# Second attention of a two-block kernel: two heads and one branch in a step, values kept stationary

## The chip, the cores and the metric

The kernel runs on one NeuronCore of a Trainium2 chip. The metric is the device time of one execution in microseconds (us). Four compute engines and a DMA system work side by side and meet only at semaphores: TensorE (PE, matrix products and transposes into the PSUM banks), VectorE (DVE), ScalarE (ACT) and GpSimd (POOL); SyncE (SP) issues the weight transfers. Each engine runs its own instructions strictly in the order in which they are written.

## The reference, cut to what matters

A first block (gated scan, attention, 16-expert layer) feeds a second block, and only the attention of the second block is touched. It works on 512 tokens with 8 query heads in 2 groups, 64 wide. Each head has three branches over the same queries: `cmp` over 31 compressed keys, `slc` over selected blocks (with 8 blocks and a top of 16, all causal keys), and `win` over a window of 512 (again all causal keys here). Scores get a distance penalty with one slope for each head, then a masked softmax, and each branch is weighted by a gate:

```python
s = jnp.einsum('bgrqd,bgqmd->bgrqm', qb, kg).astype(f32)
p_slc = masked_softmax(s - slopes * dist, dist >= 0)
o_slc = jnp.einsum('bgrqm,bgqmd->bgrqd', p_slc.astype(vg.dtype), vg)
...
o = gb[..., 0:1] * o_cmp + gb[..., 1:2] * o_slc + gb[..., 2:3] * o_win
...
mixed = jnp.concatenate([rms_norm_2(attn_out, g_out[l, :ATTN_WIDTH]),
                         rms_norm_2(conv_out, g_out[l, ATTN_WIDTH:])], axis=-1)
x = x + mixed @ w_o[l]
```

## The kernel before, in words

Everything is written by hand for each engine: `pe`, `act`, `dve`, `pool`, `sync` hold one nested function for each stage, and the stages follow one another as `second` (projections and the gated convolution), `select` (the second attention) and `ffn` (output projection `wo2`, then the feed-forward layer).

`second` computes 12 column tiles of the convolution (keys `("conv", c)`), each 24 matmuls on TensorE (L565), each with its weights split into two parts by ACT (`copy_hi`, L946) and DVE (`sub_lo`, L1415). Between them, `after` on DVE applies the norms: of the keys at tiles 0 and 1, of the queries at tiles 8 and 9.

`select` first transposes queries and keys, compresses the keys (`blkT`, L755 to L786), and then runs 32 steps, one for each block `i` of 128 queries (from the last, which sees 512 keys, to the first, which sees 128) and each head `h`. `select_order` sets for all engines where the pieces of a step stand: scores of step n, transposes of step n - 2, values of step n - 3, and at certain steps the compressed branch, the norm of the convolution (`mix_conv`) and the turning of a finished block (`turn_out`). One step is:

- PE: two matmuls (one for each branch v) of `q2T` against `kz2`, in which the other group's half is zeros (L772).
- DVE: adds slope times distance for each branch (L1954) and takes the negative row maximum (L1958).
- ACT: two exponentials with row sums (L1302).
- PE: 2(i + 1) transposes of the weights (L342); ACT copies them out (L1343).
- PE: 2(i + 1) matmuls with the transposed weights stationary and 128 value columns moving (L346).
- DVE: reciprocal of the sum times the gate (L2033, L2035) and two accumulations into `o2` (L2044).

After the eighth head of a block DVE norms the block (L2051 to L2059, with a square root on ACT), PE transposes it and DVE writes it to `mixT`, the input of `wo2`. `ffn` starts only when all three engines have ended `select`. In the text, "block" means such a block of 128 queries, called by its i.

The PSUM has 8 banks; `Banks(lo, hi)` hands them out in turn, and a taker waits for the reader of the former content.

Of the kernel before, what the change touches and what calls it, by code (L numbers as in the profile page):

```python
# [17 lines left out]
EPS = 1e-6  # L18
# [58 lines left out]
class Ring:  # L77


    def __init__(self, tensor, sems, units):  # L80
# [4 lines left out]
        for name, _, k, n in units:  # L85
            slots = [(at + s) % NS for s in range(1 if k * n <= 2048 and k <= 4 else 2)]
            at += len(slots)
            count[slots[0]] += 16
# [17 lines left out]
def cols(w, a, n):  # L106
    return w[:, a:a + n].rearrange("(k p) n -> p k n", p=128), w.shape[0] // 128, n


def weight_units(d):  # L110
# [15 lines left out]
    for p in range(8):  # L126
        for name in ("gate", "up", "down"):
            for kq in range(4):
                for e2 in range(2):
                    w = d["w_exp_" + name][2 * p + e2].rearrange("(p k) n -> p k n", k=8)  # L130
                    u.append(((name, p, kq, e2), w[:, 2 * kq:2 * kq + 2, :], 2, 1024))
# [4 lines left out]
    u += [(("wo2", s), *cols(d["w_o_2"], 512 * s, 512)) for s in range(2)]  # L136
# [12 lines left out]
def program(nc, d, out):  # L149
# [81 lines left out]
    kz2 = Area(nc, HT, DYN).take("kz2", [128, 2, 2, 512])  # L231
    m10 = Area(nc, DYN + 5216, END)
    q2T, hdn = m10.take("q2T", [128, 4, 512]), m10.take("hdn", [128, 2, 256])
    hdk, kcm = m10.take("hdk", [128, 256]), m10.take("kcm", [32, 2, 128])
    kcz, tA2 = m10.take("kcz", [128, 2, 32]), m10.take("tA2", [128, 128])
    p2, st2 = m10.take("p2", [128, 4, 2, 512]), m10.take("st2", [128, 6, 3, 2])
    cst, on = m10.take("cst", [128, 3, 8]), m10.take("on", [128, 1])
    blkT = Area(nc, m10.at, END).take("blkT", [128, 16, 2, 2, 32])
    p2T, cp = m10.take("p2T", [128, 2, 2, 512]), m10.take("cp", [128, 8, 32])
    cpT, o2 = m10.take("cpT", [32, 8, 128]), m10.take("o2", [128, 2, 512])  # L240
    o2n = m10.take("o2n", [128, 512])
# [77 lines left out]
    sec_chunks += col_chunks(("conv",), lambda u: ("conv", u), 12, 4)  # L319
    ffn_chunks = col_chunks(("wo2",), lambda u: ("wo2", u), 8, 4)  # L320
# [17 lines left out]
    def pe(T):  # L338
# [27 lines left out]
        def setup():  # L366
            b = every.take(T, "cols", dve_in["colB"])
            T.wait_ge(s_ident, 16)
            T.wait_ge(s_rows, 16 * 14)
# [187 lines left out]
        def chunk_tile(pool, key, wR, chunks, n, x, nk, freed, ready=None):  # L557
# [3 lines left out]
            for k in range(nk):  # L561
                if ready:
                    T.wait_ge(*ready(k))
                for j, (s, t) in enumerate(TERMS):
                    mm = T.matmul(b, o[s][:, k, :], x[:, t, k, :], start=(k + j == 0), stop=(k == nk - 1 and j == 2))  # L565
# [7 lines left out]
        def mix():  # L573
# [10 lines left out]
            for n, (key, *_) in enumerate(mix_chunks):  # L584
                if key[0] == "gate":
# [5 lines left out]
                    chunk_tile(pool, key, wR1, mix_chunks, n, hR1, 8, dve_mix["silu", h],  # L591
                               (lambda k: dve_mix["hR", k]) if h == 0 else None)
                elif key[0] == "mg":
                    chunk_tile(pool, key, wR1, mix_chunks, n, hR1, 8, act_mix["mg", key[1], key[2]])
                elif key[0] == "wb":
# [3 lines left out]
                    chunk_tile(pool, key, wR1, mix_chunks, n, aR, 4, dve_mix["wb", br, t])  # L599
# [3 lines left out]
                else:  # L603
# [4 lines left out]
                    chunk_tile(pool, key, wR1, mix_chunks, n, hR1, 8, dve_mix["y", t])  # L608
# [95 lines left out]
        def second():  # L704
            pool = Banks(0, 8)
            for n, (key, *_) in enumerate(sec_chunks):
                if key[0] == "raw":
                    v = key[1]
                    chunk_tile(pool, key, wR2, sec_chunks, n, hR2, 8, dve_sec["raw", v],
# [7 lines left out]
                elif key[0] == "conv":  # L717
                    chunk_tile(pool, key, wR2, sec_chunks, n, hR2, 8, dve_sec["conv", key[1]])
# [17 lines left out]
        def select():  # L736
            pool = Banks(0, 8)
            T.wait_ge(*dve_sec["qn", 1])
            for i in range(4):
                b = pool.take(T, ("q2T", i), act_sel["q2T", i])  # L740
# [3 lines left out]
            for v, src in enumerate((ksw, kww)):  # L744
                b = pool.take(T, ("k2T", v), act_sel["k2T", v])
                for i in range(4):
                    mm = turn(b[:, 128 * i:128 * i + 128], src[:, i, 0:128])
                mm.then_inc(pe_sel.sem, pe_sel.up(("k2T", v)))
            T.wait_ge(*dve_sel["blk"])
            b = pool.take(T, "hdk", act_sel["hdk"])  # L750
# [9 lines left out]
            b = pool.take(T, "hdn", act_sel["hdn"])  # L760
            T.wait_ge(*act_sel["hdk"])
            for hh in range(2):
                mm = turn(b[:, 128 * hh:128 * hh + 128], hdk[:, 128 * hh:128 * hh + 128])
# [1517 lines left out]
```

## Time and profile before

| | us |
|---|---|
| median of 3 runs | 2099.91 (2099.75 to 2102.64) |
| the profiled execution | 2094.38 |
| its span, first to last instruction | 2093.1 |
| the stretch 1481.58 to 1677.15: `select` and the first tile of `wo2` | 195.57 |
| TensorE busy over the span | 1808.2 (86%) |
| DVE / ACT busy over the span | 866.0 (41%) / 547.3 (26%) |

The profile is of one execution; its instructions carry the line of the program that wrote them. TensorE's busy time counts an instruction from its start to its modelled end, so neighbours overlap. The granted clock is 1.00 at 2.4 GHz and 0.50 at 1.2 GHz.

### The profile page before, as it was taken

The numbers are of one execution on the slowest core, as the hardware profiler recorded it, in microseconds if no ns is written. First come the engines' busy times: TensorE is split into PE (matmuls) and PEld (weight loads), VectorE is DVE, ScalarE is ACT, GpSimd is POOL, SyncE is SP. The second block draws the span as 40 slices with busy tenths as digits, with TensorE's granted clock in tenths as the row PEclk, the third lists the DMA queues.
The fourth block names the chain that finished last, engine by engine and source line by source line (L and its number), as shares of the span: only waits on it lengthen the run. The fifth ranks groups of instructions, "written<-read, shape, count | busy, mean of one in ns | idle before, by whom it ended". The sixth has DMA issues, their size and how long they took to land.

```text
span 2093.1 us, 21196 instructions
## 1 busy us (share of the span) xinstructions
PE 1808.2 (86%) x8537; PEld 1227.8 (59%) x8537; DVE 866.0 (41%) x1365; ACT 547.3 (26%) x908; POOL 126.8 (6%) x120
## 2 busy tenths in 40 slices
PE   4999889897899893888888888899788699999998
PEld 2657475766677771333232333488467678888876
DVE  4066372437733426011110111527567744444443
ACT  2134333334522313000000000232345533222221
POOL 0002120203000001000000000000000001000010
PEclk9999999998999996999999999999889899999999
DMA  9131202112104221999999999442300022232211
GB/s 348 55 109 41 82 20 101 41 72 90 41 1 167 104 98 52 384 421 421 421 422 422 421 420 420 150 156 85 121 1 1 1 81 81 82 120 81 81 41 41
DMA packets 92360, 329.44 MB, mean 157 GB/s; under 512 B 7348, under 2 KB 22632, under 8 KB 67688
## 3 DMA queue, kind: packets, MB, share of 16 engines
q1 hardware_dynamic: 84384, 312.59, 38.1%
q10 hardware_dynamic: 5928, 8.16, 1.2%
q0 software_dynamic: 1952, 7.34, 0.9%
q8 instruction: 69, 1.13, 0.2%
q14 instruction: 27, 0.22, 0.0%
HBM read 322.82 MB, written 4.19 MB: 156 GB/s over the span
## 4 chain that ended last, share of the span: by engine, by line
PE 66%; DMA 14%; DVE 12%; ACT 4%; issue 3%; ACTq 1%; POOL 1%; SPq 1%; DVEq 0%; POOLq 0%
PE PS L565 20%; PE PS L346 13%; PE PS L663 8%; PE PS L884 8%; DMA ring<-in_w_exp_down_dram 6%; DMA ring<-in_w_exp_gate_dram 5%; PE PS L342 3%; PE PS L534 3%; PE PS L674 2%; PE PS L729 2%; DVE wR L1415 1%; PE PS L772 1%; PE PS L426 1%; DMA ring<-in_w_mod_dram 1%; DVE mrow L1426 1%
## 5 line engine op out<-in xcount | busy, mean ns | idle before, releaser
L565 PE MATMUL PS<-hR,wR 128*128 128x512 f32 x1200 | 301.0, 410 | 30.9 <-DVE wR L1415 17.1
L565 PEld LDWEIGHTS PS<-hR,wR 128*128 128x128 f32 x1200 | 233.8, 197 | 95.6 <-issue 34.5
L663 PE MATMUL PS<-ring,xeT 128*64 128x512 f32 x1024 | 230.3, 600 | 40.3 <-DMA ring<-in_w_exp_gate_dram 38.0
L1415 DVE TENSOR_TENSOR wR<-ring,wR 128x1024 fp32r<-128x1024 f32 (+2 forms) x142 | 161.1, 1135 | 250.8 <-ACT wR L946 250.6
L946 ACT CAST wR<-ring 128x1024 fp32r<-128x1024 f32 (+2 forms) x142 | 138.3, 975 | 217.0 <-PE PS L884 126.5
L663 PEld LDWEIGHTS PS<-ring,xeT 128*64 128x64 f32 x1024 | 76.8, 138 | 192.5 <-issue 186.1
L884 PE MATMUL PS<-wR,hR 128*128 128x512 f32 x768 | 176.2, 390 | 8.9 <-DVE tmp L2097 6.9
L565 PE MATMUL PS<-xR,wR 128*128 128x512 f32 x768 | 175.3, 389 | 0.0
L884 PEld LDWEIGHTS PS<-wR,hR 128*128 128x128 f32 x768 | 143.6, 188 | 41.5 <-DVE tmp L2097 9.6
L565 PEld LDWEIGHTS PS<-xR,wR 128*128 128x128 f32 x768 | 144.1, 188 | 29.9
L663 PE MATMUL PS<-ring,hidT 128*64 128x512 f32 x512 | 115.2, 596 | 25.9 <-DMA ring<-in_w_exp_down_dram 20.0
L346 PE MATMUL PS<-hT,ring 128*128 128x512 f32 (+1 forms) x320 | 111.8, 508 | 4.2 <-ACT KK L1046 4.2
L663 PEld LDWEIGHTS PS<-ring,hidT 128*64 128x64 f32 x512 | 38.0, 137 | 97.9 <-issue 90.2
L346 PE MATMUL PS<-ring,hT 128*128 128x256 f32 (+1 forms) x352 | 90.5, 418 | 1.0 <-DVE hT L1475 1.0
L346 PEld LDWEIGHTS PS<-hT,ring 128*128 128x128 f32 x320 | 60.3, 190 | 53.0 <-issue 46.3
L346 PEld LDWEIGHTS PS<-ring,hT 128*128 128x128 f32 x352 | 66.6, 190 | 23.8 <-issue 15.3
L1207 ACT ACTIVATE hid<-PS 128x1024 f32<-128x1024 f32 x8 | 8.2, 1024 | 275.5 <-PE PS L663 275.5
L1832 DVE TENSOR_TENSOR hid<-hid,PS 128x1024 f32<-128x1024 f32 x8 | 9.8, 1221 | 159.5 <-ACT hid L1207 159.5
L1844 DVE TENSOR_SCALAR ye<-PS,giT 128x512 f32<-128x512 f32 x16 | 11.3, 746 | 151.4 <-PE PS L663 151.4
L2190 POOL TENSOR_TENSOR tmp<-tmp 128x512 f32<-128x512 f32 x32 | 33.3, 1042 | 524.0 <-DVE tmp L2097 524.0
L1562 DVE TENSOR_REDUCE st<-PS 128x1 f32<-128x768 f32 x32 | 30.6, 955 | 81.4 <-PE PS L427 81.4
L534 PE MATMUL PS<-Y 128*128 128x128 f32 x448 | 57.9, 285 | 6.9 <-DVE Y L1662 6.8
(381 smaller groups left out, 2316.9 us busy)
## 6 DMA issues: line engine op xcount, KB each, us to landing
ring<-in_w_exp_gate_dram SPq DMA_DIRECT2D x64, 1024.0 KB, 13.9
ring<-in_w_exp_up_dram SPq DMA_DIRECT2D x64, 1024.0 KB, 13.7
ring<-in_w_exp_down_dram SPq DMA_DIRECT2D x64, 1024.0 KB, 11.9
ring<-in_w_mod_dram SPq DMA_DIRECT2D x12, 2048.0 KB, 8.6
ring<-in_w_in_dram SPq DMA_DIRECT2D x11, 2048.0 KB, 9.3
ring<-in_w_up_dram SPq DMA_DIRECT2D x8, 2048.0 KB, 8.3
ring<-in_w_down_dram SPq DMA_DIRECT2D x8, 2048.0 KB, 7.8
ring<-in_w_in_dram SPq DMA_DIRECT2D x9, 1024.0 KB, 5.5
```

The costliest lines, as they stand in the source:

```text
L342: return T.transpose(dst, src, ident[0:k, 0:k])
L346: mm = T.matmul(dst, l, r, start=(i == 0), stop=(i == len(pairs) - 1))
L534: mm = T.matmul(b[:, 128 * x:128 * x + 128], yy, yy, start=True, stop=True)
L565: mm = T.matmul(b, o[s][:, k, :], x[:, t, k, :], start=(k + j == 0), stop=(k == nk - 1 and j == 2))
L663: mm = T.matmul(b[es, ns], stat[:, 2 * kq + k, es], W.view(units[e2])[:, k, ns], start=(kq + k == 0), stop=(kq == 3 and k == 1))
L674: T.matmul(b, ye[:, p % 2, 128 * k:128 * k + 128], PT[:, p % 2, :], start=True, stop=True) \
L729: mm = T.matmul(bs[i][:, 0:cs.stop - cs.start], hR2[:, s, kk + k, 128 * i:128 * i + 128], o[t][:, k, :], start=(kk + k + j == 0), stop=(kk ...
L884: mm = T.matmul(down[m], uR[:, r % 2, s, k, 128 * i:128 * i + 128], o[t][:, 0, 512 * q:512 * q + 512], start=(k + j == 0), stop=(k == 3 an ...
L946: A.copy(parts(wR, chunks, n)[0], W.view(unit)[:, ks, cs]).then_inc(act_hi.sem, act_hi.up(key))
L1415: V.tensor_tensor(lo, W.view(unit)[:, ks, cs], hi.bitcast(F32), ALU.subtract) \
L1562: V.tensor_reduce(st[:, n % 4, 0:1], bank(("s", n))[:, 0:768], AX, ALU.max, negate=True) \
L2190: G.tensor_tensor(tmp[:, j, :], tmp[:, j, :], tmp[:, j, :], ALU.mult) \
```

## The change

The 32 steps of `select` are made of other pieces. A step m is now a block i, a pair of heads (j of group 0 and j of group 1) and one branch v:

- PE: two matmuls with 64 contraction rows each, one for each group, on the two halves of the partitions (`kT2` without zeros), and two matmuls that add slope times distance (`slopes`, `distR`, single-pass type F32R) into the same banks. A step takes two of four banks (`four`), so two steps are in flight, and a bank pair is free when ACT has taken the exponentials.
- DVE: the maximum straight from PSUM, then, a step later, `scale`: the weights are multiplied by gate over sum before they are transposed.
- PE: the transposes as before; ACT copies them out, DVE every second one of branch 1 (half of that branch's).
- PE, once for each block: `values2`, 4(i + 1) matmuls with 64 value columns stationary and 512 columns (four heads of 128 queries) moving, plus two of the compressed branch, all summed in one bank.
- The norm over a finished block is a sum of squares on PE (`square2`); its reciprocal root is multiplied in by POOL at the end, after the last block.

`mix_conv` moves ahead of the compression; the compressed branch is asked for at other steps; the norm of the queries goes from tiles 8 and 9 to 2 and 3; `g_out` is loaded by two transfers and `wo2` by three for each unit (another order of rows); `wo2` takes the convolution's tiles first, and its first weights are split within `select`.

```diff
 def select():  # pe
...
+            def scores(m):
+                i, j, v = sel_steps[m]
                 nk = 128 * (i + 1)
+                b = four.take(T, ("s2", m), act_sel["e", m], 2)
+                for g in range(2):
+                    gs = slice(64 * g, 64 * g + 64)
+                    T.matmul(b[:, 512 * g:512 * g + nk], q2T[gs, j, 128 * i:128 * i + 128], kT2[gs, v, 0:nk],
+                             start=True, stop=False)
+                for g in range(2):
+                    mm = T.matmul(b[:, 512 * g:512 * g + nk], slopes[:, 4 * g + j, :], distR[:, 512 - nk:512],
+                                  start=False, stop=True)
+                mm.then_inc(pe_sel.sem, pe_sel.up(("s", m)))
...
+            def values2(m):
+                i = sel_steps[m][0]
+                b = pool.take(T, ("o2", i), dve_sel["mx", i])
                 T.wait_ge(*dve_sel["cpT", i])
...
                     for c in range(i + 1):
+                        for g in range(2):
+                            mm = T.matmul(b[64 * g:64 * g + 64, :], vt[:, c, 128 + 64 * g:192 + 64 * g],
+                                          pT2[v][:, c, g].rearrange("p j q -> p (j q)"), start=False,
+                                          stop=(v == 1 and c == i))
+                mm.then_inc(pe_sel.sem, pe_sel.up(("o", i)))
...
+    def select_order(scores, compress1, compress2, compress3, compressed1, compressed2, turn2, values2, square2):
+
+        for m in range(36):
+            if m < 32:
+                scores(m)
+            if m < 3:
+                (compress1, compress2, compress3)[m]()
+            if m >= 3 and (m - 3) % 8 == 7:
+                values2(m - 3)
+            if 2 <= m < 34:
+                turn2(m - 2)
+            if m < 32 and m % 8 == (3 if m < 8 else 1):
+                compressed1(sel_steps[m][0])
+            if m < 32 and m % 8 == (6 if m < 8 else 5):
+                compressed2(sel_steps[m][0])
+            if m >= 4 and (m - 4) % 8 == 7:
+                square2(sel_steps[m - 4][0])
...
-                    if c in (8, 9):
-                        if c == 8:
+                    if c in (2, 3):
+                        if c == 2:
                             V.wait_ge(*act_sec["q", 3])
...
+            def scores(m):
+                nk = 128 * (sel_steps[m][0] + 1)
+                V.wait_ge(*pe_sel["s", m])
+                V.tensor_reduce(st2[:, m % 4, 0, :], bank(("s2", m)).rearrange("p (g x) -> p g x", g=2)[:, :, 0:nk], AX,
+                                ALU.max, negate=True).then_inc(s.sem, s.up(("max", m)))
+                if m:
+                    scale(m - 1)
+
+            def scale(m):
...
+                for g in range(2):
+                    p = p2[m % 4][:, g, 0:nk]
+                    V.tensor_scalar(p, p, r[:, g:g + 1], None, ALU.mult).then_inc(s.sem, s.up())
+                s.also(("sc", m))
...
+            def values2(m):
...
+                V.wait_ge(*act_sel["sqa", i])
+                V.tensor_tensor(mixT[:, 0:4, 128 * i:128 * i + 128],
...
+    sel_steps = [(i, j, v) for i in range(3, -1, -1) for j in range(4) for v in range(2)]
```

On TensorE, in the middle of `select`, before the change, block i = 3 (`p` weights, `p2T` their transposes, `ksw` and `kww` the two branches' values):

```order
L772 MATMUL PS<-kz_143,q2T 128x512 x2
L342 MATMUL PS<-ident,p_150 128x128 x8
L346 MATMUL PS<-ksw,p2T 128x128 x4
L346 MATMUL PS<-kww,p2T 128x128 x4
L772 MATMUL PS<-kz_143,q2T 128x512 x2
L342 MATMUL PS<-ident,p_150 128x128 x8
```

The same engine after the change, where block 3 ends and block 2 has begun (`q_135` and `p2b` are the weights' buffers, `pT_148` and `pT_149` their transposes by branch):

```order
L825 MATMUL PS<-kcT,q2T 128x32 x8
L790 MATMUL PS<-kT_143,q2T 128x384 x2
L793 MATMUL PS<-distR,slopes 128x384 x2
L851 MATMUL PS<-cpT,kcm 64x512 x2
L859 MATMUL PS<-pT_148,ksw 64x512 x8
L859 MATMUL PS<-pT_149,kww 64x512 x8
L356 MATMUL PS<-ident,q_135 128x128 x6
L790 MATMUL PS<-kT_143,q2T 128x384 x2
L793 MATMUL PS<-distR,slopes 128x384 x2
L356 MATMUL PS<-ident,q_135 128x128 x6
L868 MATMUL PS<-sq,ones 128x128 x4
```

The values have gone out of the steps into one run of 18 matmuls, which stands between the scores of two steps of the next block.

On DVE, before, the end of a block (block 3's norm stands between two steps of block 2):

```order
L2044 SCALAR_TENSOR_TENSOR o_158<-PS,st_151,o_158 128x64 x2
L2051 TENSOR_TENSOR o2n<-o_158 128x512
L2053 TENSOR_REDUCE on<-o2n 128x1
L2055 TENSOR_SCALAR on<-on 128x1
L2057 RECIPROCAL on<-on 128x1
L2059 TENSOR_SCALAR o2n<-o_158,on 128x512
L1954 SCALAR_TENSOR_TENSOR p_150<-dist,PS 128x384 x2
L1958 TENSOR_REDUCE st_151<-p_150 128x2
```

On DVE after, the same place:

```order
L1978 TENSOR_REDUCE st_153<-PS 128x2
L1988 RECIPROCAL st_153<-st_153 128x2
L1990 TENSOR_TENSOR st_153<-st_153,gat 128x2
L1995 TENSOR_SCALAR q_135<-q_135,st_153 128x384 x2
L2074 TENSOR_TENSOR mixT<-PS,colA 128x4x128
L1978 TENSOR_REDUCE st_153<-PS 128x2
L1988 RECIPROCAL st_153<-st_153 128x2
L1990 TENSOR_TENSOR st_153<-st_153,gat 128x2
L1995 TENSOR_SCALAR p2b<-p2b,st_153 128x384 x2
L2064 COPY pT_149<-PS 128x3x128
L2081 TENSOR_SCALAR rinv<-PS 128x128
```

The five instructions of the norm are gone; the block's `mixT` product (L2074) stands ahead of the next step's maximum.

## Rows read from the trace of the kernel before

**Rows 1.** Busy time in the stretch: us, PE, PEld, DVE, ACT, POOL, PEclk, DMA, GB/s.

```profile
1481.58:1677.15 195.57, 152.90 (x924) 121.79 (x923) 128.43 (x324) 95.36 (x248) 0.15 (x1) 0.87 0.07 25
```

**Rows 2.** Chain that ended last, block 3: start us, us, what.

```profile
1532.33 1.72 PE PS L772 x4
1534.05 0.87 PE PS L342 x8
1534.92 1.79 PE PS L346 x16
```

**Rows 3.** A low and a high stretch; TensorE's longest wait (us, times, longest).

```profile
1508.00:1512.00 4.00, 2.52 (x12) 2.52 (x13) 0.00 (x0) 1.41 (x6) 0.00 (x0) 0.50 0.25 92
...
1588.00:1636.00 48.00, 43.22 (x317) 37.98 (x315) 38.56 (x109) 27.06 (x85) 0.00 (x0) 1.00 0.00 1
...
PE PS L342 <- DVE o2n L2059: 11.6, 4, 3.9
```

**Rows 4.** Timeline of TensorE in the experts: start us, us, line, operation, tiles.

```profile
999.45 2.74 PE L663 MATMUL PS<-ring,hidT 128*64 128x512 f32 x12
1003.29 1.08 PE L663 MATMUL PS<-ring,hidT 128*64 128x512 f32 x4 [1.10 <-DMA ring<-in_w_exp_down_dram]
```

**Rows 5.** Timeline of TensorE where a 31-row product meets a full-size one.

```profile
1576.27 1.99 PE L823 MATMUL PS<-kcm,cpT 31*128 31x64 f32 x16
...
1578.20 0.87 PE L342 MATMUL PS<-ident,p 128*128 128x128 f32 x6
```

**Rows 6.** Groups of 1480 to 1670: shapes xcount, busy us, mean ns, idle before.

```profile
L1302 ACT ACTIVATE p<-p,st 128x512 f32<-128x512 f32 x16 | 11.4, 714 | 25.2 <-DVE st L1958 25.2
...
L1958 DVE TENSOR_REDUCE st<-p 128x2 f32<-128x1024 f32 x8 | 9.8, 1220 | 0.3
...
L2033 DVE RECIPROCAL st<-st 128x2 f32<-128x2 f32 x32 | 4.9, 154 | 0.0
...
L1958 DVE TENSOR_REDUCE st<-p 128x2 f32<-128x256 f32 x8 | 3.4, 420 | 0.3
...
L2059 DVE TENSOR_SCALAR o2n<-o,on 128x512 f32<-128x512 f32 x4 | 1.9, 486 | 0.1
...
L1978 DVE TENSOR_SCALAR rinv<-PS 128x512 f32<-128x512 f32 x1 | 0.7, 692 | 7.6 <-PE PS L796 7.6
```

**Rows 7.** The same view for the first attention, whose operands lie in PSUM.

```profile
L1017 ACT ACTIVATE pb<-PS,st 128x768 f32<-128x768 f32 x32 | 28.9, 902 | 79.0 <-DVE st L1562 79.0
...
L1562 DVE TENSOR_REDUCE st<-PS 128x1 f32<-128x768 f32 x32 | 30.6, 955 | 81.4 <-PE PS L427 81.4
```

**Rows 8.** Chain through the compressed branch of block 3, first and last pieces.

```profile
1513.21 0.43 DVE cp L1998
...
1516.56 0.43 DVE cp L2018
...
1519.44 1.13 DVE cpT L2024
```

**Rows 9.** Chain: the compression, and the convolution's sum of squares.

```profile
1487.63 8.84 PE PS L755 x64
...
1547.00 5.30 PE PS L796 x8
```

**Rows 10.** Timeline from the end of `select` into `wo2`.

```profile
1666.90 1.04 ACT L946 CAST wR<-ring 128x1024 fp32r<-128x1024 f32 x1 [2.39 <-DVE mixT L1989]
...
1668.08 1.23 DVE L1415 TENSOR_TENSOR wR<-ring,wR 128x1024 fp32r<-128x1024 f32 x1 [1.34 <-ACT wR L946]
...
1670.05 12.51 PE L565 MATMUL PS<-hR,wR 128*128 128x512 f32 x48 [4.04 <-DVE hR L2073]
```

**Rows 11.** Timeline of TensorE in convolution tiles 10 and 11.

```profile
1467.49 7.33 PE L565 MATMUL PS<-hR,wR 128*128 128x512 f32 x24 [2.28 <-DVE wR L1415]
...
1475.81 5.73 PE L565 MATMUL PS<-hR,wR 128*128 128x512 f32 x24 [1.00 <-DVE wR L1415]
```

**Rows 12.** Chain at the start: issues of the small loads on ACT's queue.

```profile
5.89 0.34 ACTq L956
```

More of the change, by code:

```diff
@@ L560, in chunk_tile @@
             o = parts(wR, chunks, n)
-            for k in range(nk):
+            for k in ks:
                 if ready:
@@ L748, in select @@
                 mm.then_inc(pe_sel.sem, pe_sel.up(("k2T", v)))
+            b = early.take(T, "vc2", dve_sel["vc2"])
+            for k in range(4):
+                T.wait_ge(*act_sel["vc2", k])
+                T.matmul(b, ones, sq[:, k % 2, :], start=(k == 0), stop=(k == 3)) \
+                    .then_inc(pe_sel.sem, pe_sel.up(("vc2", k)))
             T.wait_ge(*dve_sel["blk"])
-            b = pool.take(T, "hdk", act_sel["hdk"])
+            b = early.take(T, "hdk", act_sel["hdk"])
             for v in range(2):
@@ L848, in ffn, with square2 @@
+            def square2(i):
+                b = pool.take(T, ("tot2", i), dve_sel["tot", i])
+                T.wait_ge(*act_sel["sqa", i])
+                for j in range(4):
+                    mm = T.matmul(b[:, 0:128], ones, sq[:, i % 2, 128 * j:128 * j + 128], start=(j == 0), stop=(j == 3))
+                mm.then_inc(pe_sel.sem, pe_sel.up(("tot", i)))
+            select_order(scores, compress1, compress2, compress3, compressed1, compressed2, turn2, values2, square2)
         def ffn():
@@ L1350, in select, with turn2 @@
-            select_order(scores, compress2, compress3, mix_conv, lambda i: None, compressed, turn2, values2)
+            def turn2(m):
+                i, j, v = sel_steps[m]
+                if i < 3 and j + v == 0:
+                    A.wait_ge(*pe_sel["o", i + 1])
+                for g in range(2 - v):
+                    A.wait_ge(*pe_sel["pT", m, g])
+                    A.copy(pT2[v][:, 0:i + 1, g, j, :],
+                           bank(("pT2", m, g))[:, 0:128 * i + 128].rearrange("p (c q) -> p c q", q=128)) \
+                        .then_inc(s.sem, s.up(("pT", m, g)))
@@ L2061, in select, with turn2 @@
-            select_order(scores, compress2, compress3, mix_conv, turn_out, compressed, lambda n: None, values2)
+            def turn2(m):
+                i, j, v = sel_steps[m]
+                if m == 30:
+                    scale(31)
+                if v:
+                    if i < 3 and j == 0:
+                        V.wait_ge(*pe_sel["o", i + 1])
+                    V.wait_ge(*pe_sel["pT", m, 1])
+                    V.tensor_copy(pT2[1][:, 0:i + 1, 1, j, :],
+                                  bank(("pT2", m, 1))[:, 0:128 * i + 128].rearrange("p (c q) -> p c q", q=128)) \
+                        .then_inc(s.sem, s.up(("pT", m, 1)))
@@ L2181, in pool @@
             gather(p)
-        G.wait_ge(*dve_sec["qn", 0])
-        G.memset(kz2, 0.0).then_inc(pool_sec.sem, pool_sec.up("kz2"))
         for g in (pe_mm[("conv", 11), 0], act_sec.end, dve_sec.end):
             G.wait_ge(*g)
-        G.memset(kcz, 0.0).then_inc(pool_sec.sem, pool_sec.up("kcz"))
+        for h in range(8):
+            G.tensor_scalar(slopes[:, h, :], ident, float(np.float32(2.0 ** -(h + 1))), None, ALU.mult) \
+                .then_inc(pool_sec.sem, pool_sec.up())
+        pool_sec.also("slopes")
+        G.wait_ge(*dve_sel["n2"])
+        for j in range(4):
+            G.tensor_tensor(mixT[:, j, :], mixT[:, j, :], rinv, ALU.mult).then_inc(pool_ffn.sem, pool_ffn.up(("n2", j)))
         for r in range(8):
```

411 lines of the change are left out of this document (175 added, 236 removed).

## The prediction

> **What bounds the kernel now.** I read the granted clocks first (one core), then the chain of work that ended last, then the timeline from the last convolution tile to the first tile of the output projection, because only that stretch is rewritten: 1481.58 to 1677.15, 195.6 us [rows 1]. In it TensorE is busy 152.9 us, DVE 128.4, ACT 95.4, and the mean granted clock is 0.87 [rows 1]. With two levels, 0.50 and 1.00, that is 26% of the stretch, some 51 us, at 1.2 GHz. In block 3 (512 keys) the chain stays on TensorE: 1.72 us of scores, 0.87 of transposes, 1.79 of values, 4.38 us a step [rows 2]. What breaks this are waits of TensorE at the ends of the blocks: 11.6 us in four waits for the normed block, up to 3.9 us long [rows 3]. After such waits the clock is low: 1508 to 1512, behind a wait for the compressed keys, ran at 0.50 [rows 3]. So the stretch is bound by TensorE's work in its first half, by chains through DVE at the block ends, and by the low clock behind them.
>
> **The change, TensorE's work.** The price of two half-size matmuls comes from the experts, where two 64-column products also share the array: 12 instructions in 2.74 us, and four alone, the first after a wait, in 1.08 [rows 4]. A float32 matmul is two instructions, so one of 512 columns costs 0.457 us in such a run, where a full-size one takes 1.72 / 2 = 0.86 [rows 2]. No row shows two products on the two halves of the *rows*; they could overlap likewise (0.91 us a pair) or not at all (1.72). I take 0.91, as the column pairs are the nearest row. The distance products are single-pass: 24 in 5.73 us at the full clock [rows 11], 0.24 each, 0.48 a step; new work. Transposes stay at 0.87. A step of block 3 then asks 0.91 + 0.48 + 0.87 = 2.26 us of TensorE in place of 4.38. The values come as one run for each block of 4(i + 1) + 2 matmuls: 18, 14, 10, 6 times 0.457 = 8.2, 6.4, 4.6, 2.7 us.
>
> **DVE becomes the bound of a step.** The two slope additions and two accumulations go; a maximum over 1024 numbers costs 1.22 us from SBUF [rows 6], and PSUM as source is no dearer (768 numbers 0.955 us [rows 7], against 0.95 between the two sizes of L1958). Then a reciprocal 0.154, a product of the same size, two multiplications of 512 columns at 0.486, and half a copy of 512 columns out of PSUM, for which I take the 0.69 of L1978 [rows 6]: 1.22 + 0.31 + 0.97 + 0.35, and five gaps of 0.04, 3.04 us. ACT needs 2 x 0.71 and one and a half copies, at 0.69 like DVE's, 2.46 [rows 6], and exponentials from PSUM are no dearer (768 columns 0.90 [rows 7]). The loop through two score buffers (scores 1.39, maximum 1.22, exponentials 1.42, some 4.2 us for two steps) is shorter than two DVE steps. So a step is 3.04 us, and for 384, 256 and 128 keys, with the multiplications taken linearly between 0.15 and 0.486 and the maximum between 1.22 and 0.42, it is 2.54, 2.05, 1.53. Eight of each: **73.3 us**.
>
> **What stands between the steps.** The compressed branch is three plus six small DVE instructions, 1513.21 to 1516.99 with 0.45 on ACT [rows 8], so 3.3 on DVE; then DVE waits in its order for eight transposes of TensorE (0.9) and copies 1.2 [rows 8]: 5.5 a block, **22**. The score maxima queued behind wait all that time, and TensorE for some 4.3 us of it. The values: DVE has one maximum and one `scale` left when the run begins (2.4, 2.1, 1.6 us), then waits for the run, ACT's square and its own `mixT` product, since the next maximum is queued behind: 5.8 + 4.3 + 3.0 of wait and 1.0 each for product and mean, **16**. The head: the squares' matmuls move ahead of the compression (four of 0.86 through two buffers behind ACT's copies, to about 1490.5, where the compression started at 1487.63 before); 64 compression instructions need 6.9 us at the full clock (8.84 with its low start [rows 9]); scores 1.4. **16.5** from 1481.58 to the first maximum. In return the 5.30 us run with its 4.2 us wait at 1547 [rows 9] is gone. The compressed keys' chain still delays steps 1 and 2: **4**. The tail: last transposes and copies 2.2, values 2.7, square 0.6, weight split 1.04 and 1.23 [rows 10], a quarter of a reciprocal 0.9, a difference 0.6, 24 matmuls 5.5: **14.7**. POOL's four products of 1.04 us each stand behind the convolution's tiles, which `wo2` now takes first; without that cover they would cost 4 us. Sum at the full clock: 73.3 + 22 + 16 + 16.5 + 4 + 14.7 = **147 us**.
>
> **The low clock.** TensorE keeps one wait of about 4.3 us in each block (the compressed branch), one in the head, one in the tail, and has less work between. I take as much time at 1.2 GHz as now, 50 us. There a step of block 3 takes 4.5 in place of 3.04, of block 2 3.4 in place of 2.54, of block 1 2.3 in place of 2.05, of block 0 no more; runs of values, head and tail double. About a third of 50 us is lost: **17**. The stretch becomes 164 us, a gain of 31.6. The bounds are 0 us (full clock) and 72 (all low: 20 for the steps, 22 for the values, 30 for the rest).
>
> **The edits outside.** The query norms leave DVE at convolution tiles 8 and 9, where TensorE waits 2.28 and 1.00 us and one tile runs 7.33 in place of 5.5 [rows 11], 5.1 us in all. At tiles 2 and 3 each adds 5.9 us to 1.9 of DVE work where a tile lasts 5.5; the slack there is some 2 us, so tile 5 waits about 2.7, perhaps with a low clock behind. Between 0 and 2.4 gained; I take **1**. The extra transfer of `g_out` costs one issue of 0.34 us [rows 12], and the first weight transfer waits for the last of these loads: **0.35 lost**. The additional `wo2` transfers are issued 150 us ahead of their use and cost nothing; were they late they would cost an issue of 0.4 us each, four times.
>
> The sum: 31.6 + 1 - 0.35 = 32 us. Against the profiled execution (2094.4, of which the span is 2093.1) that gives 2062; that execution ran 5.5 below the median, so against the median of 2099.9 it is **2068**.
>
> **A rule against it.** In front of and behind a product of 31 rows nothing shows: 16 instructions start 1.93 us ahead of the next full-size one [rows 5], 0.12 each, as among themselves. The Trainium skill, "TensorEngine Tiling (Array Packing)", Key Properties, says that changing the tiling mode drains the TensorE; the new step changes it twice. By the rows the sum stays at 2068; by the rule it would be the drain rival below.
>
> **The rivals.**
> - *Drain at each change of tile size.* Speaks for it: 64 changes and more, where before only the compressed branch had any. Against: [rows 5]. If a change costs the 0.15 us by which an instruction's 0.27 exceeds its 0.12 pitch, up to 10 us come on TensorE; DVE's slack hides most, 2 to 9 are left: 2070 to 2077, **2074**. 8%.
> - *The clock hardly falls.* Steps keep TensorE at work three quarters of the time, and from 1588 to 1636, TensorE being busy 43 of 48 us, the clock stayed at 1.00 [rows 3]. 147 us: **2051**. 12%.
> - *The halves don't overlap.* A step of block 3 needs 3.07 us of TensorE, equal to DVE's, some 5 us over all; 48 matmuls of values cost 0.86, 19 us more. 171 and 14 for the clock: **2089**. Against it: the experts [rows 4]. 9%.
> - *Slower: the clock stays at 1.2 GHz.* Waits in every step keep TensorE from its full clock. The stretch is 147 + 72 = 219 us: **2123**. It decides from two thirds of the stretch at 0.50 (147 + 72 x 0.67 = 195.6); before it was a quarter. Against: the value runs of up to 8 us, in which nothing waits. 5%.
>
> **How the numbers follow.** The forecast itself, with its own 2058 to 2079 (10 to 27 us lost to the clock), has 66%. The range reaches from the full clock, with some of DVE's multiplications cheaper than taken, 2048, to just past the rival without overlap, 2090. About 0.2% (4 us) is what a measurement here can tell from no change; only a mixture of lost overlap and low clock lands there, 2%; slower 5%; faster 93%.
>
> **What would show it.** Right: a step of block 3 about 3.0 us from maximum to maximum with DVE busy throughout; value runs of 8.2 us; the first `wo2` tile ending 164 us after the convolution; mean clock about 0.85 there; waits of DVE for `sqa` near 5.8 us. Wrong: pairs of 64-row products at 1.7 us; maxima from PSUM above 1.3; a mean clock below 0.7; a wait for POOL's `slopes` or `n2`.

## The result and the profile after

The changed kernel takes 2069.07 us (median of four, 2061.46 to 2070.81) against 2101.27 before: 0.9848 of the time, 95% interval 0.9829 to 0.9867. 2068 was predicted. Run once more beside the last experiments it took 2072.03 (2069.30 to 2075.02) against 2096.34 for the kernel before, 0.9883 [0.9862, 0.9904]: 24 us less there, where the first comparison has 32. The executions lie apart with the clock: 2061.5 came with a mean granted clock of 0.958, 2075.0 with 0.950. One execution each of two kernels below was in a slower state and is in no median or bracket: 3686.5 us (fillers in the blocks alone) and 2211.0 (values split). The profiled execution is the one of 2061.46 us, span 2060.1.

The rewritten stretch, from the last convolution tile to the first addition behind the first `wo2` tile, in the view of rows 1 (length, busy PE, PEld, DVE, ACT, POOL, clock, DMA, GB/s), first in this profile, then in the later one:

```profile
1480.41:1643.96 163.55, 135.08 (x716) 75.39 (x714) 110.36 (x261) 78.57 (x221) 11.85 (x12) 0.84 0.08 29
```

```profile
1483.26:1652.36 169.10, 142.19 (x716) 78.51 (x714) 110.44 (x262) 78.80 (x221) 11.83 (x12) 0.80 0.08 28
```

195.6 us at 0.87 [rows 1] have become 163.6 at 0.84. TensorE lost 18 us of work there, DVE 18. On TensorE the saving lies in the values: their matmuls (L346 and L823 before, L851 and L859 after) fell from 60.4 us of busy time to 25.8, while scores with the distance rose from 44.6 (L772) to 50.1 (L790 and L793). An undisturbed step of block 3 on DVE, timeline of the profile after (start, us, engine, line, operation, tiles):

```profile
1521.14 1.22 DVE L1978 TENSOR_REDUCE st<-PS 128x2 f32<-128x1024 f32 x1
1522.28 0.15 DVE L1988 RECIPROCAL st<-st 128x2 f32<-128x2 f32 x1
...
1522.66 0.88 DVE L1995 TENSOR_SCALAR q<-q,st 128x512 f32<-128x512 f32 x2
1523.46 0.68 DVE L2064 COPY pT<-PS 128x512 f32<-128x512 f32 x1
1524.14 1.23 DVE L1978 TENSOR_REDUCE st<-PS 128x2 f32<-128x1024 f32 x1
```

The maximum from PSUM costs 1.22, as from SBUF [rows 6]. But each instruction begins before the listed end of the one ahead: 1.14 behind the maximum's start, 0.80 behind that of two multiplications. Steps alternate between 2.32 us and, with a copy, 3.00: 2.66 on average. TensorE, same stretch and view:

```profile
1516.34 1.11 PE L790 MATMUL PS<-kT,q2T 64*128 64x512 f32 x4
1517.38 0.74 PE L793 MATMUL PS<-distR,slopes 128*128 128x512 f32 x2
1517.99 1.06 PE L356 MATMUL PS<-ident,p2b 128*128 128x128 f32 x8
1518.98 1.13 PE L790 MATMUL PS<-kT,q2T 64*128 64x512 f32 x4
```

From start to start: 1.04 for the pair of scores, 0.61 for the distance, 0.99 for the transposes, 2.64 together. So the halves do share the array (1.04, not 1.72), and TensorE needs as much as DVE. TensorE at the compressed branch and in the value run of block 3 (at the end of a row, how long it stood and for whom):

```profile
1528.58 1.87 PE L356 MATMUL PS<-ident,cp 128*32 128x128 f32 x8 [3.60 <-DVE cp L2048]
...
1542.24 1.07 PE L851 MATMUL PS<-cpT,kcm 32*64 32x512 f32 x4
1543.25 3.65 PE L859 MATMUL PS<-pT,ksw 128*64 128x512 f32 x16
1546.73 3.60 PE L859 MATMUL PS<-pT,kww 128*64 128x512 f32 x16
```

DVE at the same two places:

```profile
1530.48 1.21 DVE L2053 COPY cpT<-PS 32x1024 f32<-32x1024 f32 x1 [2.05 <-PE PS L356]
1533.64 1.22 DVE L1978 TENSOR_REDUCE st<-PS 128x2 f32<-128x1024 f32 x1 [1.95 <-PE PS L793]
...
1551.01 0.69 DVE L2074 TENSOR_TENSOR mixT<-PS,colA 128x512 f32<-128x512 f32 x1 [6.62 <-ACT sq L1367]
```

TensorE stands 3.60 us for the compressed weights, then transposes at 1.2 GHz (1.87); DVE waits for these, and for the scores behind them. The value run takes 8.0 us, and DVE waits 6.62 for its end. The same waits over all four blocks (us, times, longest):

```profile
DVE mixT L2074 <- ACT sq L1367: 16.8, 4, 6.6
...
PE PS L356 <- DVE cp L2048: 13.2, 4, 3.6
```

### The profile page after: what moved, and what is told of

Read it like the earlier page. It is cut to its first block, busy times and chain, and to the rows that moved or that the text cites. A ratio compares the mean times of both kernels' runs of the same rounds, so it can differ in the third digit from the quotient of the medians.

```text
span 2060.1 us, 20584 instructions
## 1 busy us (share of the span) xinstructions
PE 1789.1 (87%) x8329; PEld 1180.8 (57%) x8329; DVE 847.5 (41%) x1303; ACT 530.3 (26%) x881; POOL 136.4 (7%) x130
## 4 chain that ended last, share of the span: by engine, by line
PE 65%; DMA 14%; DVE 12%; ACT 4%; issue 3%; ACTq 1%; POOL 1%; SPq 1%; DVEq 0%
PE PS L579 19%; PE PS L360 12%; PE PS L678 8%; PE PS L909 8%; DMA ring<-in_w_exp_down_dram 6%; DMA ring<-in_w_exp_gate_dram 5%; PE PS L356 3%; PE PS L548 3%; PE PS L689 2%; PE PS L744 2%; DVE wR L1444 1%; PE PS L440 1%; ACT wR L963 1%; DMA ring<-in_w_mod_dram 1%; PE PS L859 1%
## 5 line engine op out<-in xcount | busy, mean ns | idle before, releaser
L360 PEld LDWEIGHTS PS<-hT,ring 128*128 128x128 f32 x320 | 60.4, 190 | 52.9 <-issue 46.3
L689 PE MATMUL PS<-PT,ye 128*128 128x512 f32 x128 | 59.2, 608 | 2.1 <-DVE PT L1875 2.1
```

Source lines behind the costliest of these rows:

```text
L360: mm = T.matmul(dst, l, r, start=(i == 0), stop=(i == len(pairs) - 1))
L689: T.matmul(b, ye[:, p % 2, 128 * k:128 * k + 128], PT[:, p % 2, :], start=True, stop=True) \
```

## The experiments

Each kernel is the changed one with one edit, or with several where the text says so (four to six executions each; numbers in brackets are the lowest and highest). They were run in three groups; the kernel before, run beside each, took 2100.0, 2098.6 and 2096.3 us, and the changed kernel itself 2069.1 and 2072.0, so a difference of 3 us or less from it says nothing. The twelve profiles begin the stretch anywhere from 1481 to 1492 us, mostly for reasons ahead of every edit, so its length stands beside the median.

### Which engine sets a step

The prediction said DVE, with 0.8 us to spare on TensorE. The rival: both, since 2.64 stands against 2.66.

```diff
-                             start=True, stop=False)
-                for g in range(2):
-                    mm = T.matmul(b[...], slopes[...], distR[...], start=False, stop=True)
+                                  start=True, stop=True)
```

> Leaves out the two distance products of each step (the slope penalty is missing from the scores). TensorE loses 0.58 us a step in block 3, 0.46, 0.35 and 0.25 in the others, 13 us of work in all, and one change between 64-row and 128-row products a step goes. If DVE alone bounds the steps: 0 to 2 us less than 2069. If TensorE bounds them: 8 to 13 less. If both need the same and each waits for the other now and then: 3 to 6 less.

2058.9 us (2057.9 to 2060.6), 10 less than the changed kernel; stretch 154.6. Maxima of block 3 on DVE without the distance products:

```profile
1521.50 1.22 DVE L1975 TENSOR_REDUCE st<-PS 128x2 f32<-128x1024 f32 x1
...
1523.82 1.22 DVE L1975 TENSOR_REDUCE st<-PS 128x2 f32<-128x1024 f32 x1
...
1526.74 1.21 DVE L1975 TENSOR_REDUCE st<-PS 128x2 f32<-128x1024 f32 x1
```

2.32 and 2.92: an undisturbed step is hardly shorter, so there DVE alone is the bound. The stretch is 9 us shorter, and most of that comes from places where DVE waits for scores, 4.2 us in all instead of 11.8: from the step with the compressed branch to the next maximum 8.20 instead of 9.50, behind the values 9.11 instead of 10.18.

```diff
-                for g in range(2):
+                for g in range(1):
                     p = p2[m % 4][:, g, 0:nk]
                     V.tensor_scalar(p, p, r[:, g:g + 1], None, ALU.mult)
```

> Leaves out the multiplication by gate over sum for the heads of group 1 (their weights stay unscaled). DVE loses one of two multiplications a step: 0.40 us of pitch in block 3, down to some 0.2 in block 0, about 9 us of work. If DVE alone bounds the steps: 7 to 9 less than 2069. If TensorE bounds them: 0 to 1 less. If both need the same: 3 to 5 less, and TensorE's clock a little higher.

Median 2059.5, in two groups: four executions at 2057 to 2060 with clocks of 0.954 to 0.960, two at 2073 to 2075 with 0.948 and 0.949. Maxima of block 3 on DVE (the profile is of the second group, but here the clock is 1.00):

```profile
1525.80 1.22 DVE L1978 TENSOR_REDUCE st<-PS 128x2 f32<-128x1024 f32 x1 [0.19 <-PE PS L793]
...
1528.40 1.23 DVE L1978 TENSOR_REDUCE st<-PS 128x2 f32<-128x1024 f32 x1 [0.58 <-PE PS L793]
...
1530.99 1.22 DVE L1978 TENSOR_REDUCE st<-PS 128x2 f32<-128x1024 f32 x1
```

Now 2.60 and 2.59: DVE waits 0.58 for TensorE, whose products there start 1.06, 0.57 and 0.96 apart, without a gap. Taking 0.8 us from DVE in two steps gained 0.12. The rival holds: both engines are full, and neither alone gives anything in these steps. What this kernel's four shorter executions won must have come elsewhere, and no profile shows where; the two longer ones, at the lower clock, have lost it again.

### What the shared array is worth

```diff
                     T.matmul(b[...], q2T[gs, ...], kT2[gs, v, 0:nk], start=True, stop=False)
-                for g in range(2):
                     mm = T.matmul(b[...], slopes[...], distR[...], start=False, stop=True)
```

> The two 64-row score products of a step no longer stand side by side: each is followed by its own distance product. Nothing is added or left out. In the profile after the change a pair of 512 columns takes 1.05 us and 1.72 is two full products one after the other, so a step of block 3 should cost TensorE up to 0.67 us more, and two further changes between 64-row and 128-row products. Theory of the prediction (DVE bounds a step at 2.65, TensorE has 0.4 to 0.8 to spare): 0 to 3 us over the 2069 of the changed kernel. Rival A (TensorE needs as much as DVE, 1.05 + 0.58 + 1.02 = 2.65 a step): 0.67, 0.5, 0.35 and 0.15 us times eight steps, 8 to 13 us more. Rival B (the halves never overlapped): no change.

2131.2 (2127.9 to 2140.1): 62 us more than the changed kernel, nearly five times the highest expectation, and 31 more than the kernel before. Its stretch and three windows of it (columns as in rows 1):

```profile
1483.26:1720.40 237.14, 213.79 (x716) 109.07 (x714) 111.58 (x261) 78.98 (x221) 11.84 (x12) 0.65 0.06 20
...
1519.00:1523.00 4.00, 4.00 (x11) 2.31 (x11) 1.25 (x2) 0.00 (x0) 0.00 (x0) 0.50 0.00 0
...
1579.00:1583.00 4.00, 4.00 (x12) 1.12 (x10) 0.00 (x0) 0.00 (x1) 0.00 (x0) 0.50 0.00 0
1583.00:1587.00 4.00, 4.00 (x22) 1.31 (x20) 0.00 (x0) 0.00 (x0) 0.00 (x0) 0.97 0.00 0
```

TensorE at the first scores, where the clock is still 1.00, and in one step of block 3:

```profile
1499.32 1.12 PE L790 MATMUL PS<-kT,q2T 64*128 64x512 f32 x2
...
1502.18 0.38 PE L356 MATMUL PS<-ident,hdk 128*128 128x128 f32 x2
...
1532.21 2.07 PE L790 MATMUL PS<-kT,q2T 64*128 64x512 f32 x2
1534.21 0.79 PE L792 MATMUL PS<-distR,slopes 128*128 128x512 f32 x1
1534.94 2.07 PE L790 MATMUL PS<-kT,q2T 64*128 64x512 f32 x2
1536.94 0.79 PE L792 MATMUL PS<-distR,slopes 128*128 128x512 f32 x1
1537.53 1.91 PE L356 MATMUL PS<-ident,p2b 128*128 128x128 f32 x8
1539.37 2.07 PE L790 MATMUL PS<-kT,q2T 64*128 64x512 f32 x2
```

No theory had this. The clock falls behind a wait of 1.86 us that ends at 1507; in most steps after it TensorE doesn't stand still by the trace, and yet the clock stays at 0.50 through them and rises only inside the run of values. A step takes 7.16 us. Its four products take 2.86 us at 1.00 (1499.32 to 1502.18) and 5.32 here, against 1.65 in the changed kernel. So two causes are mixed, the other order and the clock lost, and the clock is the larger. The next kernel has full rows (zeros in the other group's) and no sharing:

```diff
-                    T.matmul(b[...], q2T[gs, j, ...], kT2[gs, v, 0:nk], start=True, stop=False)
+                    T.matmul(b[...], q2T[:, j, ...], (kzA, kzB)[g][:, v, 0:nk], start=True, stop=False)
```

> The scores of a step are again two full-size products of 128 rows, one for each group, with zeros in the other group's rows of the keys; everything else of the change stays. So the two halves don't share the array here either, as in the kernel with the halves apart, which took 2131 us with the clock at 0.50 in nearly all its steps although TensorE never stood still in them; but here the rows are full. (ACT writes the keys in four pieces instead of two, up to 1 us in the head.) Theory A (what cost 62 us there was the clock, which doesn't rise on unpaired half-row products): the clock stays at 1.00 in the steps, a step of block 3 needs 1.72 + 0.5 + 1.0 = 3.2 us on TensorE against 2.65 now, 3 to 10 us more than 2069. Theory B (it was the overlap itself and what it does to the waits): the time lands near 2131, and the clock of the stretch near 0.65.

2069.2 (2068.9 to 2074.4), against 2072.0 for the changed kernel beside it; intervals [0.985, 0.989] and [0.9862, 0.9904]: no difference. By the clock that is theory A, though A asked for 3 to 10 us more. Its stretch:

```profile
1488.50:1655.33 166.83, 135.90 (x716) 84.35 (x714) 110.44 (x262) 79.92 (x223) 13.00 (x14) 0.90 0.08 28
```

One step of TensorE in block 3:

```profile
1529.61 1.02 PE L790 MATMUL PS<-kzA,q2T 128*128 128x512 f32 x2
1530.47 1.02 PE L790 MATMUL PS<-kzB,q2T 128*128 128x512 f32 x2
1530.93 1.03 PE L793 MATMUL PS<-distR,slopes 128*128 128x512 f32 x2
1531.80 1.03 PE L357 MATMUL PS<-ident,p2b 128*128 128x128 f32 x8
1532.67 1.02 PE L790 MATMUL PS<-kzA,q2T 128*128 128x512 f32 x2
```

Its step takes 3.06 us, the sum of 1.72, 0.47 and 0.87 (the starts inside divide it otherwise: 1.32 to the first distance product, then 0.87 and 0.87), and maxima come every 3.05 to 3.07: TensorE alone bounds it. In block 3 it is 0.4 us a step dearer, its head is 3 us longer, and still it is level: its clock is 0.90, not 0.80 to 0.84. So by these profiles, what the two halves win in the steps, the kernel gives back in the clock. And the 62 us of the halves apart are not the lost overlap, which is lost here too: they come with half-filled products, one at a time, at a clock that stays low. The kernel with the halves apart also has four changes of tile size a step, the changed one two, the one with full rows none; whether the half rows or the changes keep the clock low isn't parted.

The two steps also price a change of tile size. With full products only, the pieces add up to 3.06; with half products they should make 2.26 and make 2.64. Two changes, at most 0.38, as the 0.91 of the pair in it was an estimate. The Trainium skill, "TensorEngine Tiling (Array Packing)", Key Properties, says that changing the tiling mode drains the TensorE. The trace agrees that something is lost, up to 0.19 us a change; that it is a drain no run shows, and at the 31-row products before the change nothing was lost [rows 5].

### What the clock costs, and where

```diff
                 b = pool.take(T, ("cpT", i), dve_sel["cpT", i], 2)
+                for _ in range(12):
+                    T.matmul(b[:, 0:512], slopes[:, 0, :], distR, start=True, stop=True)
                 T.wait_ge(*dve_sel["cp", i])
```

> TensorE's four waits for the compressed weights, 3.3 us each, are filled with 12 single-pass products of 128x512 whose results are overwritten by the transposes behind them: 2.8 us of work in each wait, nothing else moves. Theory (the low clock behind these waits is what costs, and it falls because TensorE stood still): the transposes and scores behind them run at 1.00 instead of 0.50, 5 to 12 us less than 2069. Rival A (the clock falls anyway, since the steps keep TensorE too little at work): no change. Rival B (the fillers end after the weights are there): 0 to 3 us more.

2055.0 (2051.1 to 2064.6), 0.9793 [0.9769, 0.9818]: 14 us less, with more work. Its stretch:

```profile
1485.69:1637.56 151.87, 135.31 (x764) 77.68 (x762) 109.90 (x262) 78.38 (x221) 11.84 (x12) 0.94 0.09 31
```

The place that read 3.60 and 1.87 above, on TensorE:

```profile
1532.02 1.05 PE L356 MATMUL PS<-ident,cp 128*32 128x128 f32 x8 [0.72 <-DVE cp L2050]
1533.00 1.13 PE L790 MATMUL PS<-kT,q2T 64*128 64x512 f32 x4
```

The transposes take 1.05, the scores 1.13, and from 1517 to 1617 the clock is 1.00 throughout. DVE does the same as before. The waits are as long as before, only filled, so what was won is the low clock behind them. Two more kernels fill the other waits; both keep these fillers and also have POOL's earlier products, from the tail's experiment further down:

```diff
                 b = pool.take(T, ("tot2", i), dve_sel["tot", i])
+                if i == 0:
+                    for _ in range(6): T.matmul(b[:, 0:512], slopes[:, 0, :], distR, start=True, stop=True)
...
             b = pool.take(T, key, freed)
+            if key == ("wo2", 0):
+                for _ in range(3): T.matmul(b[:, 0:512], ones, xT[:, 0, :], start=True, stop=True)
```

> Three edits together: the fillers in the four waits for the compressed weights (14 us less by the run with them alone), POOL's early products (2 less by the stretch of that run), and fillers in the tail: 6 single-pass products ahead of the last sum of squares and 3 full ones ahead of the first tile of wo2, where TensorE waits 0.8 and 3.0 us and runs at 0.50 to 0.75. If the low clock of the tail comes from those waits too: the values' successor tile takes 6 instead of 10 us, 2046 to 2051. If the tail stays low all the same: 2052 to 2054. If the single gains don't add: 2055.

2058.6 (2049.8 to 2063.9), 0.982 [0.9795, 0.9844], not to be told from the fillers alone; its stretch is 149.8 against 151.9. Inconclusive by time.

```diff
             b = early.take(T, "vc2", dve_sel["vc2"])
+            for _ in range(3): T.matmul(b, ident, q2[:, 0, :], start=True, stop=True)
...
+                        for _ in range(12): T.matmul(b[:, 0:512], slopes[:, 0, :], distR, start=True, stop=True)
                         T.wait_ge(*act_sel["hdn"])
...
+                for _ in range(8): T.matmul(b[:, 0:512], slopes[:, 0, :], distR, start=True, stop=True)
                 T.wait_ge(*dve_sel["kcn"])
```

> The kernel before it and fillers in the head as well: 3 full products ahead of the convolution's sum of squares, 12 single-pass ones ahead of the compressed keys' products, 8 ahead of their transpose; TensorE waits 2.6, 3.1 and 1 to 2.4 us there, and the clock is 0.7 to 0.9 behind them. If the low clock there comes from those waits: 2 to 5 us less than with the fillers in the blocks and the tail alone. If they end too late or the clock doesn't matter there, since ACT and DVE set the pace of the head: 0 to 1 more.

2052.2 (2049.6 to 2055.9), 0.9783 [0.9763, 0.9803], beside the changed kernel's 0.9883: the lowest median of all, 20 us below it in the same comparison. The 6 us to the kernel before it in the list are not clear of the noise, as the intervals overlap. Its stretch:

```profile
1489.07:1638.71 149.64, 142.13 (x802) 83.58 (x801) 106.36 (x263) 78.09 (x221) 9.13 (x12) 0.98 0.09 32
```

### Order at the block ends, and the tail

`compressed3` holds TensorE's transposes and DVE's copy:

```diff
             if m < 32 and m % 8 == (6 if m < 8 else 5):
                 compressed2(sel_steps[m][0])
+            if m % 8 == (0 if 8 <= m < 9 else 7) and m > 7:
+                compressed3(sel_steps[m - 2][0])
```

> The eight transposes of the compressed weights, and DVE's copy of them, move two steps later, so that TensorE doesn't wait for DVE's six small instructions and DVE doesn't wait for the transposes. After the change TensorE waits 13.2 us there in four waits and DVE 7.4 us for the copy's source; the stretches at the low clock stand right behind (1528, 1561, 1592, 1613 us and on). Theory (the price of the compressed branch beyond its 3.3 us is these waits, and the low clock comes from them): 10 to 20 us less than 2069, waits of both gone, mean clock of the stretch above 0.90. Rival (DVE's small instructions delay the next maximum all the same, so TensorE waits for that instead and the clock falls as before): 0 to 5 less.

2062.0 (2049.7 to 2062.5), 7 us less; stretch 156.1 at 0.86. TensorE's wait for `cp` is gone and DVE's for the transposes fell from 7.4 to 2.0 us. But new waits of TensorE for the multiplied weights came, up to 2.0 us, and the clock still fell behind them: between theory and rival.

`values1` has the compressed and the selected branch, `values2` the window branch:

```diff
             if m >= 3 and (m - 3) % 8 == 7:
-                values2(m - 3)
+                values1(m - 3)
+            if m in (11, 19, 27, 34):
+                values2(min(m // 8 * 8, 32) - 1)
```

> The run of values of a block is cut in two: compressed and selected branch first, the window branch one step later, with that step's scores and transposes between. DVE waits 16.8 us in four waits for such a run (the longest 6.6), because it holds only one step's work in hand. Theory: for three blocks DVE can work off one more step beside the runs, 2.3 + 1.9 + 1.5, so 4 to 6 us less than 2069, and DVE's longest wait for the sum of squares falls from 6.6 to below 4. Rival (each half leaves DVE as long a wait as it now hides): 0, or 1 us more for the extra changes of tile size.

2072.0 (2067.9 to 2077.3): no gain, the rival. DVE's waits (us, times, longest):

```profile
DVE st L1987 <- PE PS L793: 20.7, 16, 4.7
...
DVE mixT L2083 <- ACT sq L1376: 6.8, 4, 2.2
```

The wait for the square fell from 16.8 to 6.8, that for scores rose from 11.8 to 20.7: each half keeps DVE without scores as long as the whole did.

```diff
-        G.wait_ge(*dve_sel["n2"])
+        G.wait_ge(*dve_sel["n2a"])
         for j in range(4):
-            G.tensor_tensor(mixT[:, j, :], mixT[:, j, :], rinv, ALU.mult)
+            G.tensor_tensor(mixT[:, j, 128:512], mixT[:, j, 128:512], rinv[:, 128:512], ALU.mult)
```

> In the tail POOL multiplies the columns of blocks 3 to 1 as soon as their reciprocal roots are there, beside the last run of values, and DVE multiplies only the 128 columns of block 0; before that POOL multiplied all 512 columns after the last root, at 1.66 us a slice, with ACT waiting for each, and DVE's differences took 1.2 instead of 0.69 beside it. Theory: the first tile of wo2 is no longer paced by POOL, 2 to 4 us less than 2069. Rival (TensorE at the low clock needs its 10 us for that tile anyway): 0 to 1 less.

2067.6 (2063.0 to 2068.8): 1.5 less by the median, within the spread; the stretch is 161.5, 2.0 shorter, and from the last maximum on it is 22.7 instead of 24.0. The tail of the changed kernel, DVE's differences, POOL's products and the first products of `wo2`:

```profile
1633.50 9.16 DVE L2099 TENSOR_TENSOR hR<-mixT,hR 128x512 fp32r<-128x512 f32 x8
1633.67 6.64 POOL L2216 TENSOR_TENSOR mixT<-mixT,rinv 128x512 f32<-128x512 f32 x4 [146.12 <-DVE rinv L2086]
...
1634.27 6.29 PE L579 MATMUL PS<-hR,wR 128*128 128x512 f32 x12 [3.01 <-DVE hR L2099]
```

The same in this kernel:

```profile
1630.61 3.86 POOL L2221 TENSOR_TENSOR mixT<-mixT,rinv 128x384 f32<-128x384 f32 x4 [139.30 <-DVE rinv L2073]
...
1637.06 4.90 DVE L2104 TENSOR_TENSOR hR<-mixT,hR 128x512 fp32r<-128x512 f32 x8
```

Beside each other POOL's products take 1.68 us each and the four of DVE's differences between them 1.75 (the other four 0.62 to 0.69, so the eight average 1.21); apart, DVE's all take 0.69, and POOL's 1.00 for three quarters of the columns. The Trainium skill, "SBUF — State Buffer", "SBUF: two separate sides", says that a DVE operation with two SBUF inputs and a GpSimd operation that reads SBUF take turns on one port pair. The trace agrees: 1.68 and 1.75 are each close to the sum of the two alone, 0.69 and the 1.04 of POOL's other products of 512 columns. Only 1.4 us of it reach the end of `wo2`'s first tile.

### Outside the stretch, and the control

```diff
-                    if c in (2, 3):
+                    if c in (8, 9):
```

> The norm of the queries goes back to convolution tiles 8 and 9, the rest of the change stays. Prediction: 1 us more than the changed kernel (0 to 2.4). By the two profiles, where the convolution's twelve tiles took 70.8 us before and 67.9 after: 2.9 us more, and TensorE's waits of 2.3 and 1.0 us ahead of tiles 10 and 11 come back.

2072.9 (2065.3 to 2077.2): 1 to 4 us more, within the spread. The trace is clearer: the waits ahead of tiles 10 and 11 are back, 2.27 and 2.63 us, and the twelve tiles, from the first matmul to the last addition, take 72.5 us against 68.1 and 69.7 in the two profiles of the changed kernel.

> The changed kernel itself, with nothing altered, beside the others of this call: 2069 us by its four executions (2061.5 to 2070.8). It says how far its executions lie apart on this chip, and whether its stretch of 163.6 us is the rule; the differences of 2 to 4 us among the kernels here are read against it.

2072.0, as told above, stretch 169.1. Its 5.6 us over the first profile are clock: the middle takes 125.7 us instead of 120.1, head and tail the same. Four windows of it in blocks 1 and 0:

```profile
1600.00:1604.00 4.00, 4.00 (x22) 2.89 (x20) 2.73 (x12) 2.54 (x13) 0.00 (x0) 0.50 0.01 2
1604.00:1608.00 4.00, 4.00 (x27) 2.96 (x26) 2.67 (x10) 1.49 (x8) 0.00 (x0) 0.50 0.00 0
1608.00:1612.00 4.00, 4.00 (x12) 1.00 (x10) 0.38 (x2) 0.49 (x4) 0.00 (x0) 0.50 0.00 0
1612.00:1616.00 4.00, 4.00 (x17) 1.25 (x13) 0.07 (x1) 0.70 (x3) 0.00 (x0) 0.71 0.00 0
```

The clock fell in a wait of 3.17 us ahead of these windows; in them TensorE has no pause by the trace, and it rises only in the value run (from 1608). In the first profile the same wait is 3.16 us, and there the clock is back at 1.00 by 1600, in the steps, ahead of that block's value run. The program is the same; why the clock came back sooner isn't shown.

## Why the prediction was right, step by step

The sum at the full clock can be held against the kernel with all waits filled, whose clock is 0.98 (its tail also has POOL's earlier products):

| term | predicted | measured, clock held | why |
|---|---|---|---|
| head | 16.5 | 17.8 | its parts, 8.9, 6.9 and 1.4, make 17.2; measured 8.9, 7.1, 1.8 |
| steps | 73.3 | 62.6 | DVE's instructions overlap at their ends |
| compressed branch | 22 | 23.8 | four times 4.3 to 4.8, and 1.2 to 1.7 ahead |
| value waits | 16 | 20.3 | 8.1, 6.1, 4.1, and 0.5 to 0.8 each for the mean |
| compressed keys | 4 | 5.1 | 13.1 for three intervals, less 8.0 |
| tail | 14.7 | 19.6 | POOL and DVE slow each other; fillers |
| sum | 147 | 149.6 | |
| low clock | 17 | 13.9 and 19.5 | 163.6 and 169.1 less 149.6 |

The measured terms are differences between maxima: an interval with the extra work less an undisturbed one of its block, with or without the copy as it has one (2.66, 2.22, 1.70, 1.25 us on average); they add up to within 1 us. Of the low clock's 14 to 20 us, some 2 are POOL's. The sum was right by luck: one term too high by 10.7 us, the steps, met five too low by some 13 together. The forecast's own range was said as 10 to 27 us lost to the clock; added to 2051 these give 2061 to 2078, not 2058 to 2079.

- *DVE's step* was mis-sized: 3.04, 2.54, 2.05, 1.53 predicted, 2.66, 2.22, 1.70, 1.25 measured. I added the listed lengths and 0.04 of gap for each of five; the starts lie 0.08 closer than the lengths (1.14 behind a 1.22 maximum).
- *TensorE's step* was mis-sized the other way, 2.64 instead of 2.26. The 0.38 is near the price of the drain rival (0.15 a change, two a step), which got 8%. In the undisturbed steps DVE's 2.66 hides it, as that rival said, but with nothing to spare. The rival's 2070 to 2077 holds the second median, 2072, so the time doesn't tell it from the forecast; what the step shows is its price. The pair itself overlapped, as taken from the experts' column pairs [rows 4].
- *DVE as the bound* was half right: without the distance products, and with half the multiplications, both engines turned out full.
- *The values*: 8.03 us for the run of block 3, 8.2 predicted; waits of 6.6, 5.0 and 3.5, with 5.8, 4.3 and 3.0 predicted.
- *The low clock*: 0.84 is 52 us at 1.2 GHz, 50 were taken, and it cost 14 to 20. That the waits at the block ends bring it was shown by filling them. That the value runs keep the slower rival away holds only in part: with the halves apart, and in blocks 1 and 0 of the second profile, the clock rises there alone. In the first profile it is back at 1.00 in the steps, from 1536 in the row below, 6 us ahead of the run at 1542. That rival, the clock staying low through the steps, is what the kernel with the halves apart shows, at 2131; 2123 was its price.

```profile
1536.00:1540.00 4.00, 3.73 (x26) 2.39 (x24) 3.86 (x11) 3.27 (x10) 0.00 (x0) 1.00 0.00 0
```

- *Halves that don't overlap*: 2089 was its price, some 5 us of the difference for the scores. The kernel with full rows takes the overlap from the scores alone and is no slower. The step that failed there: full products were charged for their length and not credited for the clock.
- *Edits outside*: the first product with a loaded weight starts 1.0 us later, not 0.35; the convolution is 1.3 to 2.9 shorter, 1 predicted. Together 0.3 to 1.9 gained, where 0.65 was said.
- *POOL's* `slopes` delayed nothing, as said; its last products did, with waits of 4.5 us on ACT, which the text had set at no cost behind the convolution's tiles. A wait for `n2` was one of its signs of being wrong, and here it is right: the tail is the term that it mis-sized, 14.7 for 19.6.

How the 32 us divide between the values' new form and the additions taken from DVE wasn't run apart; TensorE's busy time, above, shows only that the work saved there is the values'. It stays open also why the clock stays low on a TensorE that the trace shows busy.

## What to carry to other kernels

Count an engine's step from start to start in the trace, not by adding lengths, and then ask whether the other engine in the loop has just become equal: there the next gain on either one is next to nothing. Before TensorE waits some 3 us for another engine, give it products whose result is thrown away, in a bank that it holds anyway; here that, with some 2 us from POOL's earlier products, was worth 20 us of 2072, more than half of what the change itself brought. A product on half the rows needs its partner beside it at once; here even the pair was no faster than full rows with zeros.

## What was not expected of the hardware

- TensorE, busy for 4.00 of 4.00 us by the trace in window after window, kept a granted clock of 0.50 through nearly all steps when its 64-row products ran one at a time, and in the changed kernel itself, run again, from 1596 to 1612 us. There it rose in the runs of values; in the first profile of the changed kernel it rose in the steps.
- A change between 64-row and 128-row products costs up to 0.19 us.
- POOL's product and DVE's difference side by side take 1.68 and 1.75 us; without the other DVE's takes 0.69.
